# Layer 0's dense experts loaded as pairs of blocks of 1 MB, with the ring of gathered rows cut from 16 places to 14

## The chip, the cores and the metric

The kernel runs on one core of one Trainium2 chip. The metric is the device time of one execution in microseconds. A program on one core has that core as its slowest, so nothing is averaged over cores.

## What is computed

A diffusion backbone of two layers works on 256 latent tokens and 256 context tokens of 1024 features in float32. Each layer is a parallel mixer (two gated scans, two attentions) and then a feed-forward of 16384 small experts (PEER). Of the latter each token takes 8 x 16 = 128 experts:

```python
def peer_ffn(h, w_q, keys, u, v):
    ...
        best, sel = lax.top_k(cand, PEER_TOPK)
        eidx = jnp.take_along_axis(cidx, sel, axis=-1)
        g = jax.nn.softmax(best, axis=-1)
        act = jax.nn.gelu(jnp.einsum('td,thkd->thk', xb, u[eidx]).astype(jnp.float32))
        return jnp.einsum('thk,thkd->td', (g * act).astype(v.dtype), v[eidx]).astype(h.dtype)
```

In layer 0 this is done for the 256 context tokens and the 256 latent tokens, in layer 1 for the latent tokens alone.

## The kernel before

The change lies in `phase_mixed`, the feed-forward of layer 0, which runs two kinds of work beside each other.

**Dense, for the latent tokens.** All 16384 experts are gone through in 128 blocks of 128 experts. A block of `u` is 512 KB (`us`, 128 partitions x 1024 float32), and so is a block of `v` (`vs`). For block e: ScalarE copies the block to a rounded high part (`u_high`, L2328), VectorE subtracts to get the low part (`u_low`, L2363), TensorE makes 24 products (`hidden`), ScalarE applies gelu (L2337), VectorE multiplies by the gates (L2375) and makes another low part (L2382), the block of `v` is split in the same way (ScalarE L2346, VectorE L2384), and TensorE adds 24 products to the output (`outputs`). Each of `us` and `vs` has SW = 3 places of one block. The gates of four blocks come as one more transfer of 512 KB (L2235), in runs of 1 KB.

**Sparse, for the context tokens.** There are 512 gathers of 128 rows of 4 KB (512 KB each), listed in `order` and issued by GpSimd (L2251) into `ring`, which has R = 16 places. A row set of `u` is multiplied and summed by VectorE (a "dot", L2389). Four row sets of `v` together are used by TensorE in one "quad" (L2300). The list starts with the 128 `u` sets of token tile 0. Then come three `u` sets of tile 1 and one `v` set of tile 0 in turn, and then `v` sets alone. Slot s of the list may be gathered when slot s - R has been consumed.

All engines go through 132 steps. In step k TensorE does hidden(k), outputs(k - 2) and then, if one is due, a quad. VectorE does wt(k - 1), u_low(k + 1), wl and vl(k - 1), and then the dots of the four slots that belong to step k - 2 (PER = 4, LAG = 2). The first quad is due in step 37. In the part in which `u` and `v` sets alternate, one quad is due in every fourth step from there (37, 41, 45 and so on), and in the part with `v` sets alone one is due in each step.

SyncE's queue carries the dense loads in program order (L2229 u, L2235 gates, L2238 v), each behind a wait for the place it writes. It and GpSimd's queue share the core's 16 DMA engines.

The waits that matter for the order are these:

```python
if e >= SW:
    sp.wait_ge(vlo, e - SW + 1)
sp.dma_start(vs[:, e % SW], d["v_rows"][e * P:(e + 1) * P]).then_inc(v_in[e % SW], 16)
...
if s >= R:
    pool.wait_ge(*consumed(s - R))
```

Of the kernel before, what the change touches and what calls it, by code (L numbers as in the profile page):

```python
# [110 lines left out]
def f32(ap):  # L111

    return ap.bitcast(F32)
# [28 lines left out]
def build(nc, d, out):  # L142
# [14 lines left out]
    def sb(st, name, shape, dt=F32):  # L157
        return st.enter_context(nc.sbuf_tensor(name, shape, dt))

    with ctx:  # L160
# [1972 lines left out]
        def phase_mixed(l, hp, hT, eid, eidT, gate):  # L2133
# [6 lines left out]
            R = 16  # L2140
            PER = 4
            LAG = 2
            SW = 3
# [52 lines left out]
            with ExitStack() as st:  # L2196
                us = sb(st, f"peer_u{l}", [P, SW, DC, P])
                uh = sb(st, f"peer_uh{l}", [P, 2, DC, P], F32R)
                ul = sb(st, f"peer_ul{l}", [P, 2, DC, P], F32R)
                vs = sb(st, f"peer_v{l}", [P, SW, D_MODEL])  # L2200
# [22 lines left out]
                with nc.Block() as block:  # L2223
                    @block.sync
                    def _(sp):
                        for e in range(NKEY):
                            if e >= SW:
                                sp.wait_ge(ulo, e - SW + 1)
                            sp.dma_start(us[:, e % SW], d["uT"][e]).then_inc(u_in[e % SW], 16)  # L2229
                            if e % GROWS == 0:  # L2230
                                b = e // GROWS
                                if b >= 2:
                                    sp.wait_ge(w_done, GROWS * (b - 1))
                                src = gates_dram[0:ntb, :, e:e + GROWS, :].rearrange("b p i t -> p b (i t)")
                                sp.dma_start(gs[:, b % 2].rearrange("p b i t -> p b (i t)"), src).then_inc(g_in[b % 2], 16)  # L2235
                            if e >= SW:
                                sp.wait_ge(vlo, e - SW + 1)
                            sp.dma_start(vs[:, e % SW], d["v_rows"][e * P:(e + 1) * P]).then_inc(v_in[e % SW], 16)  # L2238
# [84 lines left out]
                    def _(act):  # L2323
                        def u_high(e):
                            act.wait_ge(u_in[e % SW], 16 * (e // SW + 1))
                            if e >= 2:
                                act.wait_ge(act_mm, e - 1)
                            nc.scalar.activation(uh[:, e % 2], us[:, e % SW], ACT.Copy).then_inc(uhi, 1)  # L2328

                        u_high(0)  # L2330
                        for step in range(steps + 1):
# [8 lines left out]
                            if 0 <= e < NKEY:  # L2340
                                act.wait_ge(w_done, e + 1)
                                if e >= 2:
                                    act.wait_ge(out_mm, e - 1)
                                nc.scalar.activation(wh[:, e % 2], wt[:, e % 2], ACT.Copy).then_inc(whi, 1)
                                act.wait_ge(v_in[e % SW], 16 * (e // SW + 1))
                                nc.scalar.activation(vh[:, e % 2], vs[:, e % SW], ACT.Copy).then_inc(vhi, 1)  # L2346
# [13 lines left out]
                    def _(dve):  # L2360
                        def u_low(e):
                            dve.wait_ge(uhi, e + 1)
                            nc.vector.tensor_tensor(ul[:, e % 2], us[:, e % SW], f32(uh[:, e % 2]), ALU.subtract).then_inc(ulo, 1)  # L2363

                        u_low(0)
                        for step in range(steps + 1):
# [13 lines left out]
                            if 0 <= e < NKEY:  # L2380
                                dve.wait_ge(whi, e + 1)
                                nc.vector.tensor_tensor(wl[:, e % 2], wt[:, e % 2], f32(wh[:, e % 2]), ALU.subtract).then_inc(wlo, 1)  # L2382
                                dve.wait_ge(vhi, e + 1)
                                nc.vector.tensor_tensor(vl[:, e % 2], vs[:, e % SW], f32(vh[:, e % 2]), ALU.subtract).then_inc(vlo, 1)  # L2384
# [127 lines left out]
def lay_out(x, c, ctx, c_ctx, ada_w, ada_b, norm_mix_g, norm_ffn_g, w_in, w_out,  # L2512
# [34 lines left out]
    a["uT"] = peer_u[0].reshape(NKEY, P, DC, P).transpose(0, 3, 2, 1)  # L2547
# [21 lines left out]
```

## Time and profile before

| | |
|---|---|
| median of 3 runs | 3184.79 us (3181.0 to 3188.43) |
| the profiled execution, its own time | 3183.49 us |
| its span | 3181.7 us |
| mean granted TensorE clock | 0.888 |
| TensorE matmul busy | 2546.1 us (80%) |
| VectorE busy | 2022.4 us (64%) |
| `phase_mixed` in the span | from about 980 to about 2045 us |

The page has a digit for each fortieth of the span (79.5 us): busy tenths of each engine, the granted clock and the busy share of the DMA engines. A share a little over 1 in the windows means that records of packets overlap.

### The profile page before, as it was taken

The page shows a single profiled execution, that of the slowest core. Times are in us where ns is not written, and L with a number is a line of the kernel's source. Part 1 is how long each engine was busy: PE and PEld are TensorE (multiplying, and loading weights), DVE is VectorE, ACT ScalarE, POOL GpSimd, SP SyncE. Part 2 cuts the span into 40 slices and gives each one's busy share as a digit, 9 for nine tenths or more (in the row PEclk, how much of TensorE's full clock was granted, in tenths as well). Part 3 has the DMA queues.
Part 4 walks back from the last instruction along what each step waited for, and adds up shares of the span by engine and source line. Part 5 has one row for each costly group of instructions (what it writes and reads, how often), then busy time and mean ns, then how long its engine had stood idle before and what let it go on. Part 6 is the DMA issues. An engine that isn't in the chain of part 4 may idle for free. (4 is left out here: it accounts for less than half of the span.)

```text
span 3181.7 us, 41584 instructions
## 1 busy us (share of the span) xinstructions
PE 2546.1 (80%) x15562; PEld 1903.4 (60%) x15562; DVE 2022.4 (64%) x4495; ACT 1084.4 (34%) x2179; POOL 1119.1 (35%) x1013
## 2 busy tenths in 40 slices
PE   5978699797376778878799999888877797777776
PEld 3778445595165777767777777577746553222222
DVE  3566435489995989887844333467543699845444
ACT  3422235321073333333333333342234443333332
POOL 1024100331005667556665555212302354433431
PEclk8985589897698989999999999988678899999999
DMA  5210141135238999999999999621002799999996
GB/s 208 74 30 1 62 159 42 53 113 180 106 152 325 405 407 404 363 401 385 402 406 406 405 406 406 263 87 43 9 1 85 303 391 422 421 421 422 421 422 258
DMA packets 211897, 816.93 MB, mean 257 GB/s; under 512 B 22681, under 2 KB 41689, under 8 KB 178033
## 3 DMA queue, kind: packets, MB, share of 16 engines
q0 software_dynamic: 110592, 536.92, 41.7%
q1 hardware_dynamic: 101104, 277.35, 23.4%
q8 instruction: 124, 2.03, 0.3%
q14 instruction: 77, 0.62, 0.1%
HBM read 796.37 MB, written 17.83 MB: 256 GB/s over the span
## 5 line engine op out<-in xcount | busy, mean ns | idle before, releaser
L1919 PE MATMUL ps<-pair_ring,pair_diag 128*128 128x512 f32 x1024 | 476.3, 610 | 144.8 <-ACT pair_diag L1993 142.2
L2103 DVE CUSTOM_DVE_ANT_0 pair_ring<-pair_ring,hT 128x1024 f32<-128x1024 f32 x256 | 312.9, 1222 | 206.7 <-DMA pair_ring<-in_uv_rows,eid 206.7
L1919 PEld LDWEIGHTS ps<-pair_ring,pair_diag 128*128 128x128 f32 x1024 | 187.1, 192 | 423.3 <-ACT pair_diag L1993 228.5
L1883 POOL DMA_INDIRECT pair_ring<-in_uv_rows,eid x256 | 268.2, 1048 | 391.9 <-PE ps L1919 364.0
L2251 POOL DMA_INDIRECT sparse_ring<-in_v_rows,eidT x256 | 279.5, 1092 | 298.4 <-PE ps L2300 226.9
L2251 POOL DMA_INDIRECT sparse_ring<-in_u_rows,eid x256 | 339.4, 1326 | 122.5 <-issue 68.1
L118 PE MATMUL ps<-h_hi,peer_uh 128*128 128x256 f32 x1024 | 310.1, 303 | 85.6 <-DVE peer_ul L2363 77.9
L2389 DVE CUSTOM_DVE_ANT_0 sparse_ring<-sparse_ring,hT 128x1024 f32<-128x1024 f32 x256 | 304.7, 1224 | 41.9 <-DMA sparse_ring<-in_u_rows,eid 35.7
L120 PE MATMUL ps<-h_hi,peer_ul 128*128 128x256 f32 x1024 | 299.2, 292 | 1.1 <-issue 0.9
L119 PE MATMUL ps<-h_lo,peer_uh 128*128 128x256 f32 x1024 | 299.4, 292 | 0.1
L118 PEld LDWEIGHTS ps<-h_hi,peer_uh 128*128 128x128 f32 x1024 | 206.0, 201 | 149.4 <-DVE peer_ul L2363 92.0
L118 PE MATMUL ps<-peer_wh,peer_vh 128*128 128x256 f32 x1024 | 291.3, 285 | 1.8 <-issue 1.7
L119 PE MATMUL ps<-peer_wl,peer_vh 128*128 128x256 f32 x1024 | 290.5, 284 | 0.4 <-issue 0.3
L120 PE MATMUL ps<-peer_wh,peer_vl 128*128 128x256 f32 x1024 | 290.1, 283 | 0.1
L2363 DVE TENSOR_TENSOR peer_ul<-peer_u,peer_uh 128x1024 fp32r<-128x1024 f32 x128 | 156.5, 1223 | 164.3 <-ACT peer_uh L2328 132.7
L2328 ACT ACTIVATE peer_uh<-peer_u 128x1024 fp32r<-128x1024 f32 x128 | 135.2, 1057 | 292.2 <-DMA peer_u<-in_uT 273.7
L120 PEld LDWEIGHTS ps<-h_hi,peer_ul 128*128 128x128 f32 x1024 | 206.2, 201 | 1.3 <-issue 1.3
L119 PEld LDWEIGHTS ps<-h_lo,peer_uh 128*128 128x128 f32 x1024 | 206.6, 202 | 0.2 <-issue 0.2
L118 PEld LDWEIGHTS ps<-peer_wh,peer_vh 128*128 128x128 f32 x1024 | 197.8, 193 | 2.6 <-issue 2.4
L119 PEld LDWEIGHTS ps<-peer_wl,peer_vh 128*128 128x128 f32 x1024 | 197.5, 193 | 2.1 <-issue 2.1
L120 PEld LDWEIGHTS ps<-peer_wh,peer_vl 128*128 128x128 f32 x1024 | 197.2, 193 | 0.8 <-issue 0.8
L2300 PE MATMUL ps<-sparse_ring,sparse_wdiag 128*32 128x512 f32 x1024 | 137.2, 653 | 67.2 <-DMA sparse_ring<-in_v_rows,eidT 66.2
(397 smaller groups left out, 5411.5 us busy)
## 6 DMA issues: line engine op xcount, KB each, us to landing
peer_u<-in_uT SPq DMA_DIRECT2D x128, 512.0 KB
peer_v<-in_v_rows SPq DMA_DIRECT2D x128, 512.0 KB
ada_slab<-in_ada_w SPq DMA_DIRECT2D x20, 2048.0 KB, 8.6
proj_slab<-in_w_fm SPq DMA_DIRECT2D x38, 512.0 KB
route_slab<-in_w_pq SPq DMA_DIRECT2D x32, 512.0 KB, 3.3
peer_gates<-dense_stage SPq DMA_DIRECT2D x4, 4096.0 KB, 13.1
peer_gates<-peer_gates SPq DMA_DIRECT2D x32, 512.0 KB
out_slab<-in_w_out SPq DMA_DIRECT2D x16, 512.0 KB, 3.7
```

The lines of the kernel that those rows point to most:

```text
L118: nc.tensor.matmul(out, w[0], x[0], start=start, stop=False)
L119: nc.tensor.matmul(out, w[0], x[1], start=False, stop=False)
L120: return nc.tensor.matmul(out, w[1], x[0], start=False, stop=stop)
L1883: nc.gpsimd.indirect_dma_start(out=ring[:, s % R], out_offset=None, in_=d["uv_rows"], in_offset=bass.IndirectOffsetOnAxis(ap=eid[:, s:s + ...
L1919: mm = nc.tensor.matmul(ps[:, 4 + 2 * t + half, :], diag[:, s % DG, :], ring[:, s % R, D_MODEL + half * BANK:D_MODEL + (half + 1) * BANK], ...
L2103: nc.vector.tensor_tensor_reduce(out=row, in0=row, in1=hT[:, s // NS], scale=1.0, scalar=0.0, op0=ALU.mult, op1=ALU.add, accum_out=dots[:, ...
L2251: nc.gpsimd.indirect_dma_start(out=ring[:, s % R], out_offset=None, in_=rows, in_offset=bass.IndirectOffsetOnAxis(ap=at, axis=0)).then_inc ...
L2300: mm = nc.tensor.matmul(ps[32 * q:32 * (q + 1), 6 + half, :], wdiag[:, q, j, :], ring[:, s % R, half * BANK:(half + 1) * BANK], start=(j = ...
L2328: nc.scalar.activation(uh[:, e % 2], us[:, e % SW], ACT.Copy).then_inc(uhi, 1)
L2363: nc.vector.tensor_tensor(ul[:, e % 2], us[:, e % SW], f32(uh[:, e % 2]), ALU.subtract).then_inc(ulo, 1)
L2389: nc.vector.tensor_tensor_reduce(out=ring[:, s % R], in0=ring[:, s % R], in1=hT[:, t], scale=1.0, scalar=0.0, op0=ALU.mult, op1=ALU.add, a ...
```

## The change

A block of `u` and the block after it become one transfer of 1 MB that writes 8 KB in each partition, and the same for `v`. For that the host lays `uT` out by pairs and adds an input `v_pairs` (the gathers go on reading `v_rows`). `us` and `vs` have two places of a pair each where they had three places of a block. So they take 8 KB more per partition in all, and the ring of gathered rows, 4 KB a place, gives these up: R is 14. SyncE waits until both blocks of the pair two before have been used. The arithmetic is the same.

```diff
-            R = 16
+            R = 14
...
-            SW = 3
+            SW = 2
...
-                us = sb(st, f"peer_u{l}", [P, SW, DC, P])
+                us = sb(st, f"peer_u{l}", [P, SW, 2, DC, P])
...
-                vs = sb(st, f"peer_v{l}", [P, SW, D_MODEL])
+                vs = sb(st, f"peer_v{l}", [P, SW, 2, D_MODEL])
...
-                        for e in range(NKEY):
-                            if e >= SW:
-                                sp.wait_ge(ulo, e - SW + 1)
-                            sp.dma_start(us[:, e % SW], d["uT"][e]).then_inc(u_in[e % SW], 16)
-                            if e % GROWS == 0:
-                                b = e // G**Rows 1.** The page, busy share in 40 slices of the span.

```profile
DMA  5210141135238999999999999621002799999996
GB/s 208 74 30 1 62 159 42 53 113 180 106 152 325 405 407 404 363 401 385 402 406 406 405 406 406 263 87 43 9 1 85 303 391 422 421 421 422 421 422 258
```

**Rows 2.** DMA of 980:2045, all of `phase_mixed`: queue, packets, MB, share of 16 engines.

```profile
DMA packets 127569, 420.62 MB, mean 395 GB/s; under 512 B 12800, under 2 KB 29184, under 8 KB 127488
...
q0 software_dynamic: 73728, 268.47, 63.6%
q1 hardware_dynamic: 53760, 151.01, 36.4%
```

**Rows 3.** Windows: us, busy (instructions) by engine, clock, DMA share, GB/s.

```profile
1064.00:1264.00 200.00, 156.50 (x1170) 152.24 (x1169) 183.90 (x292) 63.99 (x96) 135.50 (x97) 0.92 1.03 405
1300.00:1400.00 100.00, 81.02 (x621) 72.60 (x620) 83.33 (x125) 32.24 (x48) 60.11 (x49) 0.91 1.03 404
1400.00:1500.00 100.00, 80.67 (x624) 71.76 (x623) 79.48 (x120) 32.58 (x48) 59.74 (x48) 0.91 1.00 388
...
1800.00:1900.00 100.00, 95.53 (x778) 74.49 (x777) 38.12 (x48) 32.65 (x48) 51.56 (x51) 1.00 1.03 406
```

**Rows 4.** DMA of 2690:3100, layer 1, where gathered rows have 8 KB.

```profile
DMA packets 23716, 172.77 MB, mean 421 GB/s; under 512 B 2632, under 2 KB 2632, under 8 KB 2632
```

**Rows 5.** DMA of 1306:1322, between two transfers of gates, runs of 4 KB.

```profile
DMA packets 1798, 6.56 MB, mean 410 GB/s; under 512 B 199, under 2 KB 199, under 8 KB 1797
```

**Rows 6.** DMA of 616:640, with one transfer of 1024 KB over 128 partitions.

```profile
DMA packets 700, 3.06 MB, mean 128 GB/s; under 512 B 80, under 2 KB 80, under 8 KB 572
...
route_keys<-in_keysT SPq DMA_DIRECT2D x1, 1024.0 KB, 8.3
```

**Rows 7.** DMA of 1552:1554 and of 1556:1558, each queue's share.

```profile
q0 software_dynamic: 113, 0.41, 51.7%
q1 hardware_dynamic: 113, 0.40, 49.9%
...
q0 software_dynamic: 171, 0.61, 77.1%
q1 hardware_dynamic: 48, 0.20, 24.4%
```

**Rows 8.** Waits of 1060:1240: who waited for whom, us, times, longest.

```profile
ACT peer_uh L2328 <- DMA peer_u<-in_uT: 88.3, 22, 8.0
```

**Rows 9.** Window of 1284:1300, before the first quad, columns as in Rows 3.

```profile
1284.00:1300.00 16.00, 16.00 (x128) 14.43 (x128) 15.57 (x24) 7.40 (x12) 2.54 (x3) 0.95 0.56 193
```

**Rows 10.** Timelines of ACT, POOL, PE and SP, start us, us, [idle before <- releaser].

```profile
984.76 1.06 ACT L2328 ACTIVATE peer_uh<-peer_u 128x1024 fp32r<-128x1024 f32 x1 [17.52 <-DMA peer_u<-in_uT]
...
1296.85 0.95 POOL L2251 DMA_INDIRECT sparse_ring<-in_v_rows,eidT  x1 [20.53 <-PE ps L2300]
...
1315.94 1.93 POOL L2251 DMA_INDIRECT sparse_ring<-in_v_rows,eidT  x1 [0.30 <-issue]
...
1330.86 0.94 POOL L2251 DMA_INDIRECT sparse_ring<-in_v_rows,eidT  x1 [9.04 <-PE ps L2300]
...
1327.30 3.26 PE L2300 MATMUL ps<-sparse_ring,sparse_wdiag 128*32 128x512 f32 x16 [7.54 <-DMA sparse_ring<-in_v_rows,eidT]
...
1329.84 0.33 SPq L2238 DMA_DIRECT2D peer_v<-in_v_rows  x1
...
1595.39 0.94 POOL L2251 DMA_INDIRECT sparse_ring<-in_v_rows,eidT  x1 [8.61 <-PE ps L2300]
```

**Rows 11.** DMA of 1332:1334 and of 1334:1336, just after that quad.

```profile
q1 hardware_dynamic: 389, 0.75, 103.7%
q0 software_dynamic: 10, 0.03, 4.3%
...
q1 hardware_dynamic: 143, 0.49, 62.3%
q0 software_dynamic: 73, 0.29, 36.4%
```
-                                if b >= 2:
-                                    sp.wait_ge(w_done, GROWS * (b - 1))
-                                src = gates_dram[0:ntb, :, e:e + GROWS, :].rearrange("b p i t -> p b (i t)")
-                                sp.dma_start(gs[:, b % 2].rearrange("p b i t -> p b (i t)"), src).then_inc(g_in[b % 2], 16)
-                            if e >= SW:
-                                sp.wait_ge(vlo, e - SW + 1)
-                            sp.dma_start(vs[:, e % SW], d["v_rows"][e * P:(e + 1) * P]).then_inc(v_in[e % SW], 16)
+                        for b in range(NKEY // 2):
+                            if b >= SW:
+                                sp.wait_ge(ulo, 2 * (b - SW + 1))
+                            sp.dma_start(us[:, b % SW], d["uT"][b]).then_inc(u_in[b % SW], 16)
+                            if 2 * b % GROWS == 0:
+                                x = 2 * b // G**Rows 1.** The page, busy share in 40 slices of the span.

```profile
DMA  5210141135238999999999999621002799999996
GB/s 208 74 30 1 62 159 42 53 113 180 106 152 325 405 407 404 363 401 385 402 406 406 405 406 406 263 87 43 9 1 85 303 391 422 421 421 422 421 422 258
```

**Rows 2.** DMA of 980:2045, all of `phase_mixed`: queue, packets, MB, share of 16 engines.

```profile
DMA packets 127569, 420.62 MB, mean 395 GB/s; under 512 B 12800, under 2 KB 29184, under 8 KB 127488
...
q0 software_dynamic: 73728, 268.47, 63.6%
q1 hardware_dynamic: 53760, 151.01, 36.4%
```

**Rows 3.** Windows: us, busy (instructions) by engine, clock, DMA share, GB/s.

```profile
1064.00:1264.00 200.00, 156.50 (x1170) 152.24 (x1169) 183.90 (x292) 63.99 (x96) 135.50 (x97) 0.92 1.03 405
1300.00:1400.00 100.00, 81.02 (x621) 72.60 (x620) 83.33 (x125) 32.24 (x48) 60.11 (x49) 0.91 1.03 404
1400.00:1500.00 100.00, 80.67 (x624) 71.76 (x623) 79.48 (x120) 32.58 (x48) 59.74 (x48) 0.91 1.00 388
...
1800.00:1900.00 100.00, 95.53 (x778) 74.49 (x777) 38.12 (x48) 32.65 (x48) 51.56 (x51) 1.00 1.03 406
```

**Rows 4.** DMA of 2690:3100, layer 1, where gathered rows have 8 KB.

```profile
DMA packets 23716, 172.77 MB, mean 421 GB/s; under 512 B 2632, under 2 KB 2632, under 8 KB 2632
```

**Rows 5.** DMA of 1306:1322, between two transfers of gates, runs of 4 KB.

```profile
DMA packets 1798, 6.56 MB, mean 410 GB/s; under 512 B 199, under 2 KB 199, under 8 KB 1797
```

**Rows 6.** DMA of 616:640, with one transfer of 1024 KB over 128 partitions.

```profile
DMA packets 700, 3.06 MB, mean 128 GB/s; under 512 B 80, under 2 KB 80, under 8 KB 572
...
route_keys<-in_keysT SPq DMA_DIRECT2D x1, 1024.0 KB, 8.3
```

**Rows 7.** DMA of 1552:1554 and of 1556:1558, each queue's share.

```profile
q0 software_dynamic: 113, 0.41, 51.7%
q1 hardware_dynamic: 113, 0.40, 49.9%
...
q0 software_dynamic: 171, 0.61, 77.1%
q1 hardware_dynamic: 48, 0.20, 24.4%
```

**Rows 8.** Waits of 1060:1240: who waited for whom, us, times, longest.

```profile
ACT peer_uh L2328 <- DMA peer_u<-in_uT: 88.3, 22, 8.0
```

**Rows 9.** Window of 1284:1300, before the first quad, columns as in Rows 3.

```profile
1284.00:1300.00 16.00, 16.00 (x128) 14.43 (x128) 15.57 (x24) 7.40 (x12) 2.54 (x3) 0.95 0.56 193
```

**Rows 10.** Timelines of ACT, POOL, PE and SP, start us, us, [idle before <- releaser].

```profile
984.76 1.06 ACT L2328 ACTIVATE peer_uh<-peer_u 128x1024 fp32r<-128x1024 f32 x1 [17.52 <-DMA peer_u<-in_uT]
...
1296.85 0.95 POOL L2251 DMA_INDIRECT sparse_ring<-in_v_rows,eidT  x1 [20.53 <-PE ps L2300]
...
1315.94 1.93 POOL L2251 DMA_INDIRECT sparse_ring<-in_v_rows,eidT  x1 [0.30 <-issue]
...
1330.86 0.94 POOL L2251 DMA_INDIRECT sparse_ring<-in_v_rows,eidT  x1 [9.04 <-PE ps L2300]
...
1327.30 3.26 PE L2300 MATMUL ps<-sparse_ring,sparse_wdiag 128*32 128x512 f32 x16 [7.54 <-DMA sparse_ring<-in_v_rows,eidT]
...
1329.84 0.33 SPq L2238 DMA_DIRECT2D peer_v<-in_v_rows  x1
...
1595.39 0.94 POOL L2251 DMA_INDIRECT sparse_ring<-in_v_rows,eidT  x1 [8.61 <-PE ps L2300]
```

**Rows 11.** DMA of 1332:1334 and of 1334:1336, just after that quad.

```profile
q1 hardware_dynamic: 389, 0.75, 103.7%
q0 software_dynamic: 10, 0.03, 4.3%
...
q1 hardware_dynamic: 143, 0.49, 62.3%
q0 software_dynamic: 73, 0.29, 36.4%
```
+                                if x >= 2:
+                                    sp.wait_ge(w_done, GROWS * (x - 1))
+                                src = gates_dram[0:ntb, :, 2 * b:2 * b + GROWS, :].rearrange("b p i t -> p b (i t)")
+                                sp.dma_start(gs[:, x % 2].rearrange("p b i t -> p b (i t)"), src).then_inc(g_in[x % 2], 16)
+                            if b >= SW:
+                                sp.wait_ge(vlo, 2 * (b - SW + 1))
+                            sp.dma_start(vs[:, b % SW], d["v_pairs"][b]).then_inc(v_in[b % SW], 16)
...
-                            act.wait_ge(u_in[e % SW], 16 * (e // SW + 1))
+                            act.wait_ge(u_in[e // 2 % SW], 16 * (e // 2 // SW + 1))
...
-                            nc.scalar.activation(uh[:, e % 2], us[:, e % SW], ACT.Copy).then_inc(uhi, 1)
+                            nc.scalar.activation(uh[:, e % 2], us[:, e // 2 % SW, e % 2], ACT.Copy).then_inc(uhi, 1)
...
-    a["uT"] = peer_u[0].reshape(NKEY, P, DC, P).transpose(0, 3, 2, 1)
+    a["uT"] = peer_u[0].reshape(NKEY // 2, 2, P, DC, P).transpose(0, 4, 1, 3, 2)
+    a["v_pairs"] = peer_v[0].reshape(NKEY // 2, 2, P, D_MODEL).transpose(0, 2, 1, 3)
```

The other lines of the diff (L2346, L2363, L2384) only address the block inside its pair.

SyncE's program at the start of `phase_mixed` (`in_uT` is the input of `u`, `in_v_rows` that of `v`, `peer_gates` the gates), four blocks of it before:

```order
L2229 DMA peer_u<-in_uT 128x1024
L2235 DMA peer_gates<-peer_gates 128x4x256
L2238 DMA peer_v<-in_v_rows 128x1024
L2229 DMA peer_u<-in_uT 128x1024
L2238 DMA peer_v<-in_v_rows 128x1024
L2229 DMA peer_u<-in_uT 128x1024
L2238 DMA peer_v<-in_v_rows 128x1024
L2229 DMA peer_u<-in_uT 128x1024
L2238 DMA peer_v<-in_v_rows 128x1024
```

The same queue at the same place after the change:

```order
L2229 DMA peer_u<-in_uT 128x2048
L2235 DMA peer_gates<-peer_gates 128x4x256
L2238 DMA peer_v<-in_v_pairs 128x2048
L2229 DMA peer_u<-in_uT 128x2048
L2238 DMA peer_v<-in_v_pairs 128x2048
```

Four blocks take five transfers where they took nine, and the gates stand behind a pair of `u` and ahead of a pair of `v`. The programs of TensorE, VectorE and ScalarE have the same instructions in the same order, and so has GpSimd's; its waits look 14 slots back instead of 16.

## Rows read from the trace of the kernel before

**Rows 1.** The page, busy share in 40 slices of the span.

```profile
DMA  5210141135238999999999999621002799999996
GB/s 208 74 30 1 62 159 42 53 113 180 106 152 325 405 407 404 363 401 385 402 406 406 405 406 406 263 87 43 9 1 85 303 391 422 421 421 422 421 422 258
```

**Rows 2.** DMA of 980:2045, all of `phase_mixed`: queue, packets, MB, share of 16 engines.

```profile
DMA packets 127569, 420.62 MB, mean 395 GB/s; under 512 B 12800, under 2 KB 29184, under 8 KB 127488
...
q0 software_dynamic: 73728, 268.47, 63.6%
q1 hardware_dynamic: 53760, 151.01, 36.4%
```

**Rows 3.** Windows: us, busy (instructions) by engine, clock, DMA share, GB/s.

```profile
1064.00:1264.00 200.00, 156.50 (x1170) 152.24 (x1169) 183.90 (x292) 63.99 (x96) 135.50 (x97) 0.92 1.03 405
1300.00:1400.00 100.00, 81.02 (x621) 72.60 (x620) 83.33 (x125) 32.24 (x48) 60.11 (x49) 0.91 1.03 404
1400.00:1500.00 100.00, 80.67 (x624) 71.76 (x623) 79.48 (x120) 32.58 (x48) 59.74 (x48) 0.91 1.00 388
...
1800.00:1900.00 100.00, 95.53 (x778) 74.49 (x777) 38.12 (x48) 32.65 (x48) 51.56 (x51) 1.00 1.03 406
```

**Rows 4.** DMA of 2690:3100, layer 1, where gathered rows have 8 KB.

```profile
DMA packets 23716, 172.77 MB, mean 421 GB/s; under 512 B 2632, under 2 KB 2632, under 8 KB 2632
```

**Rows 5.** DMA of 1306:1322, between two transfers of gates, runs of 4 KB.

```profile
DMA packets 1798, 6.56 MB, mean 410 GB/s; under 512 B 199, under 2 KB 199, under 8 KB 1797
```

**Rows 6.** DMA of 616:640, with one transfer of 1024 KB over 128 partitions.

```profile
DMA packets 700, 3.06 MB, mean 128 GB/s; under 512 B 80, under 2 KB 80, under 8 KB 572
...
route_keys<-in_keysT SPq DMA_DIRECT2D x1, 1024.0 KB, 8.3
```

**Rows 7.** DMA of 1552:1554 and of 1556:1558, each queue's share.

```profile
q0 software_dynamic: 113, 0.41, 51.7%
q1 hardware_dynamic: 113, 0.40, 49.9%
...
q0 software_dynamic: 171, 0.61, 77.1%
q1 hardware_dynamic: 48, 0.20, 24.4%
```

**Rows 8.** Waits of 1060:1240: who waited for whom, us, times, longest.

```profile
ACT peer_uh L2328 <- DMA peer_u<-in_uT: 88.3, 22, 8.0
```

**Rows 9.** Window of 1284:1300, before the first quad, columns as in Rows 3.

```profile
1284.00:1300.00 16.00, 16.00 (x128) 14.43 (x128) 15.57 (x24) 7.40 (x12) 2.54 (x3) 0.95 0.56 193
```

**Rows 10.** Timelines of ACT, POOL, PE and SP, start us, us, [idle before <- releaser].

```profile
984.76 1.06 ACT L2328 ACTIVATE peer_uh<-peer_u 128x1024 fp32r<-128x1024 f32 x1 [17.52 <-DMA peer_u<-in_uT]
...
1296.85 0.95 POOL L2251 DMA_INDIRECT sparse_ring<-in_v_rows,eidT  x1 [20.53 <-PE ps L2300]
...
1315.94 1.93 POOL L2251 DMA_INDIRECT sparse_ring<-in_v_rows,eidT  x1 [0.30 <-issue]
...
1330.86 0.94 POOL L2251 DMA_INDIRECT sparse_ring<-in_v_rows,eidT  x1 [9.04 <-PE ps L2300]
...
1327.30 3.26 PE L2300 MATMUL ps<-sparse_ring,sparse_wdiag 128*32 128x512 f32 x16 [7.54 <-DMA sparse_ring<-in_v_rows,eidT]
...
1329.84 0.33 SPq L2238 DMA_DIRECT2D peer_v<-in_v_rows  x1
...
1595.39 0.94 POOL L2251 DMA_INDIRECT sparse_ring<-in_v_rows,eidT  x1 [8.61 <-PE ps L2300]
```

**Rows 11.** DMA of 1332:1334 and of 1334:1336, just after that quad.

```profile
q1 hardware_dynamic: 389, 0.75, 103.7%
q0 software_dynamic: 10, 0.03, 4.3%
...
q1 hardware_dynamic: 143, 0.49, 62.3%
q0 software_dynamic: 73, 0.29, 36.4%
```

More of the change, by code:

```diff
@@ L2225, in _ @@
                     def _(sp):
-                        for e in range(NKEY):
-                            if e >= SW:
-                                sp.wait_ge(ulo, e - SW + 1)
-                            sp.dma_start(us[:, e % SW], d["uT"][e]).then_inc(u_in[e % SW], 16)
-                            if e % GROWS == 0:
[L2231 to L2238, printed above, removed]
+                        for b in range(NKEY // 2):
+                            if b >= SW:
+                                sp.wait_ge(ulo, 2 * (b - SW + 1))
+                            sp.dma_start(us[:, b % SW], d["uT"][b]).then_inc(u_in[b % SW], 16)
+                            if 2 * b % GROWS == 0:
+                                x = 2 * b // GROWS
+                                if x >= 2:
+                                    sp.wait_ge(w_done, GROWS * (x - 1))
+                                src = gates_dram[0:ntb, :, 2 * b:2 * b + GROWS, :].rearrange("b p i t -> p b (i t)")
+                                sp.dma_start(gs[:, x % 2].rearrange("p b i t -> p b (i t)"), src).then_inc(g_in[x % 2], 16)
+                            if b >= SW:
+                                sp.wait_ge(vlo, 2 * (b - SW + 1))
+                            sp.dma_start(vs[:, b % SW], d["v_pairs"][b]).then_inc(v_in[b % SW], 16)
                     @block.gpsimd
@@ L2324, in u_high @@
                         def u_high(e):
-                            act.wait_ge(u_in[e % SW], 16 * (e // SW + 1))
+                            act.wait_ge(u_in[e // 2 % SW], 16 * (e // 2 // SW + 1))
                             if e >= 2:
                                 act.wait_ge(act_mm, e - 1)
-                            nc.scalar.activation(uh[:, e % 2], us[:, e % SW], ACT.Copy).then_inc(uhi, 1)
+                            nc.scalar.activation(uh[:, e % 2], us[:, e // 2 % SW, e % 2], ACT.Copy).then_inc(uhi, 1)
                         u_high(0)
@@ L2344, in _ @@
                                 nc.scalar.activation(wh[:, e % 2], wt[:, e % 2], ACT.Copy).then_inc(whi, 1)
-                                act.wait_ge(v_in[e % SW], 16 * (e // SW + 1))
-                                nc.scalar.activation(vh[:, e % 2], vs[:, e % SW], ACT.Copy).then_inc(vhi, 1)
+                                act.wait_ge(v_in[e // 2 % SW], 16 * (e // 2 // SW + 1))
+                                nc.scalar.activation(vh[:, e % 2], vs[:, e // 2 % SW, e % 2], ACT.Copy).then_inc(vhi, 1)
                             for t in range(nt):
@@ L2546, in lay_out @@
     a["keysT"] = peer_keys.reshape(DEPTH, 2 * PH, NKEY, P).transpose(0, 3, 1, 2)
-    a["uT"] = peer_u[0].reshape(NKEY, P, DC, P).transpose(0, 3, 2, 1)
+    a["uT"] = peer_u[0].reshape(NKEY // 2, 2, P, DC, P).transpose(0, 4, 1, 3, 2)
+    a["v_pairs"] = peer_v[0].reshape(NKEY // 2, 2, P, D_MODEL).transpose(0, 2, 1, 3)
     a["u_rows"] = peer_u[0]
```

4 lines of the change are left out of this document (2 added, 2 removed).

## The prediction

> **What bounds the kernel now.** I read the page first for the slices of `phase_mixed`, then the DMA queues of that stretch, then windows by stage, and last the waits and the timeline around the places where the DMA is not full. Between 980 and 2045 us the busy digit of the DMA engines is 9 in nearly every slice, at 401 to 407 GB/s where nothing dips [rows 1]. In that stretch they move 420.62 MB at a mean of 395 GB/s, 63.6% of their time for the gathers (q0) and 36.4% for SyncE's loads (q1) [rows 2]. VectorE is busy 184 of 200 us early and 38 of 100 us late, while the DMA share stays at 1.03 and the rate at 405 or 406 GB/s [rows 3]. So neither VectorE nor TensorE sets the pace of the whole phase. The bytes do: 420.62 MB at 406 GB/s are 1036 us of about 1065. A change pays here if it makes the bytes move faster or shortens the 29 us in which they don't move. It costs if it opens new gaps. I look for nothing outside this phase, since nothing else is edited.
>
> **The runs of 8 KB: -8.6 us.** In layer 1, where a gathered row has 8 KB, 421 GB/s are moved [rows 4]. Here, with runs of 4 KB in both queues and no gates in flight, it is 410 GB/s [rows 5]. SyncE's queue can make such runs too: with one transfer of 1024 KB over 128 partitions, 700 - 572 = 128 packets had 8 KB or more [rows 6]. The blocks of `u` and `v` are 256 x 0.524 = 134.2 MB. At 410 GB/s they take 327.4 us, at 421 GB/s 318.8 us, so 8.6 us are saved. The bounds are 0 (the packets stay at 4 KB, or the gathers' rate holds the pair back) and about 2 x 8.6 (the other queue gains as well). I take 8.6, since both rows are long and full. The Trainium skill ("DMA: Bandwidth & Descriptors", section "Why small descriptors are slow") charges some 3 cycles per packet beside one cycle per 32 bytes, which makes 259 cycles for 8 KB against 262 for two of 4 KB: by that 1.1%, an estimate of 3.7 us where the rows give 8.6. The rows differ by 2.7%, so I stay with them.
>
> **Fewer waits for u: nothing by itself.** ScalarE waits 88.3 us of 180 for a block of `u` [rows 8]. The reason is in how the queues share. With runs of 4 KB in both they have half each, and while gates in runs of 1 KB are on their way q0 has 77.1% and q1 24.4% [rows 7]. Those gates stand ahead of the next blocks in q1. With runs of 8 KB q1 should have two thirds while its blocks move, and the gates now come at the end of a burst, with nothing behind them for two steps. So u will be early and these waits should nearly go. But the DMA is full during them [rows 3], so what `u` gains the gathered rows lose: VectorE will wait for them instead. I cost this at 0, covered by the full DMA, with one exception, which is next. By the Trainium skill (same page, "Queues, rings and completion order") an engine goes round its queues packet by packet; the halves and the 77 to 24 above agree with that.
>
> **The gap before the first quad: -6 us.** From 1284 to 1300 only 193 GB/s are moved, that is (1 - 193/408) x 16 = 8.4 us of DMA time unused [rows 9]. All that the rings allow had landed: GpSimd stood 20.53 us until 1296.85 for the quad of step 37 [rows 10], and the engines were late because of the waits for `u` before. Now VectorE follows the gathers. The last slot of that quad (143) should land at about 1283 as before, since the DMA was always full up to 1284; with 3.3 us of quad [rows 10] GpSimd can go on at about 1288 instead of 1297. Some 8.5 us are won, of which two sets fewer in the ring take back 2 x 0.524 MB / 410 GB/s = 2.6 us. I take -6. The bounds are -8.4 (the gap gone) and +2.6 (engines as late as now, and two sets fewer landed).
>
> **The ring of 14 while u and v alternate: +18 us.** A quad takes slots that lie four apart, so its first place is held long: slot 147 cannot be gathered before the quad of step 37 is done, and with 14 places it is slot 145. Each such round of four steps runs as follows now. GpSimd resumes at T = 1330.86 after 9.04 us idle [rows 10]. The gathers move again only at about T + 3.7: they have 4.3% of 1332 to 1334 and 36.4% of the next 2 us, at half rate the last 1.4 us of these [rows 11]. In between q1 fills the engines (103.7%) with the load issued at 1329.84 and the gates before it [rows 10, 11]. The next quad needs the 13th set issued after the resumption before (issued at 1315.94, awaited until 1327.30). Nine rounds, from 1296.85 to 1595.39, are 33.2 us each [rows 10]; the bytes of a round, 25 x 0.524 = 13.1 MB, need 32.3 us at 406 GB/s. So the gap of q0 is nearly covered today, because the two sets issued before the stop are still on their way at T. With 14 places they are not issued. The gap begins 2.6 us sooner, and the quad needs 15 sets after T. What covers it is worse placed, too: the gates come with the burst two steps before (15 us), not one, and the pair's burst starts to move only some 3 us after its issue, at about T + 2. A round is then 3.7 us to the restart, 15 sets and 3.5 to 4.0 MB of dense loads at 412 GB/s (27.6 to 28.8 us), and 3.5 us for landing and quad: 34.8 to 36.0 us, or 1.6 to 2.8 more than 33.2. The bounds are 0 (pairs, whose two places hold a block more each, cover the gap wholly) and 2.8. I take 2.0, nearer the lower end of the working, since part of a burst may still be behind the quad's last set; nine rounds make +18 us. This already has the faster runs of the rounds, so of the 8.6 us above only what lies outside them is counted: 720 of 1065 us, -5.8.
>
> **The late part and the ends.** With `v` sets alone a quad frees four places in each step, and ten sets are still issued when TensorE waits for one; the DMA has always work: 0. ScalarE starts at 984.76 once the first 512 KB of `u` are there [rows 10]; 1 MB needs 0.524 / 0.41 = 1.3 us more. GpSimd fills the ring meanwhile, so I take +1, between 0 and +2.6. SyncE issues 128 loads fewer; its queue stands waiting most of the time: 0.
>
> **Sum.** -5.8 - 6 + 18 + 1 = +7.2 us. The profiled execution took 3183.5 us, 1.3 less than the median of the runs, 3184.8. So 3190.7 there, and 3192.0 for a median. A measurement of this kernel can tell about 0.2% (6.4 us) from no change, and 7.2 us is 0.23%: just outside.
>
> **Rivals.**
> - *The dense bursts cover the gap (faster).* Two places of a pair hold one block more than three places of a block, for `u` and for `v`, exactly what the ring lost. A burst is due in every second step and a quad in every fourth, and VectorE's burst of step k + 1 falls just at T, so 2 MB wait there where 1 MB did. The dips of today (388 GB/s in 1400 to 1500 [rows 3]) could then even shrink. For it: q1 covers the gap today [rows 11]. Against it: q1 will be done sooner after each burst. The third term is then 0 and the first whole: -8.6 - 6 + 1 = -13.6, about 3171; with the first gap unchanged, -7.6, about 3177.
> - *Rows starved by the bursts (slower, more than forecast).* At T the two sets that VectorE needs next meet a burst of 2 MB that takes two thirds. Each set then takes 0.524 / 0.137 = 3.8 us, and VectorE stands some 7 us per round. It has about 28 us of work in a round of 33 (83% [rows 3]), so with 7 us of standing it needs 35 us and from there on it decides itself. If that adds 1 us to the 2.8 in nine rounds, the sum is -5.8 - 3 + 34 + 1 = +26, 3211.
> - *No runs of 8 KB.* If the loads are cut to 4 KB, the rate stays and the queues go on sharing by halves: the first terms go, and the ring's remains, about +12 to +18, 3200. Rows 6 speak against it.
> - *The terms cancel.* With 1 us more per round in place of 2 (+9) the sum is -2, 3183.
>
> **How the numbers follow.** The forecast case, +3 to +20 us, has 0.35; starved rows 0.08; no long runs 0.03; terms that cancel 0.26; covered gaps 0.28. The part of the first under 6.4 us (0.06) counts as the same, as does 0.01 of the covered case. So faster 0.27, same 0.33, slower 0.40. The range reaches from the covered case to past the forecast: 3171 to 3207, with one tenth left out on each side. The forecast case's own range is 3188 to 3205.
>
> **What would show it.** Right steps: 512 packets of 8 KB per four blocks in q1 (two pairs of u, two of v) and a rate of 412 to 416 GB/s where the DMA is full; ScalarE's wait for `u` nearly gone and VectorE's wait for gathered rows in its place; GpSimd released for the first time near 1288 to 1290; then rounds of about 35 us with a hole of some 3 us in the DMA just before and after each release. Wrong: rounds of 33 us or less without a hole (the bursts cover it, and the kernel is faster), the rate at 406, or VectorE full between 1300 and 1600 us.

## The result and the profile after

In the diff of SyncE's program the two lines that break off at `G` divide by the number of blocks whose gates come in one transfer, four: `e // 4` before and `2 * b // 4` after.

The median of 7 runs is 3198.18 us (3190.47 to 3219.98), where 7 runs of before gave 3184.79 us (3181.0 to 3188.43). The ratio of after to before is 1.0057, with a 95% interval of 1.003 to 1.0084. The span of the profiled execution is 3194.8 us, before 3181.7.

The change makes the kernel slower: by 13.4 us between the medians, by 0.57% (18 us) in the ratio, which the slowest of its runs pull up, and by 13.1 us between the two profiled executions. The runs of after spread over 30 us, those of before over 7.

Put on the time axis, the 13.1 us split at three marks. GpSimd's first release by a quad comes at 1289.26 us (before 1296.85 [rows 10]): -7.6. Its release nine rounds later comes at 1614.31 (before 1595.39 [rows 10]), so a round takes (1614.31 - 1289.26) / 9 = 36.1 us in place of 33.2: +26.5 over nine. From there to the first addition of the outputs (L1349, at 2041.58 before and at 2058.44 now) -2.1 us are won, and in the rest of the kernel, where nothing was edited, -3.8. That rest took from 1134.8 to 1142.7 us in the thirteen profiled executions of this case, whatever the kernel, so -3.8 says nothing of the change. The marks in the timelines after the change:

| mark | engine | start, us | idle before, us | ended by |
|---|---|---|---|---|
| first release by a quad | GpSimd (L2251) | 1289.26 | 24.43 | TensorE's quad (L2300) |
| release nine rounds later | GpSimd (L2251) | 1614.31 | 10.81 | TensorE's quad (L2300) |
| first addition of the outputs | VectorE (L1349) | 2058.44 | 7.15 | TensorE's products (L120) |

The windows by stage after the change, from the same view as [rows 3]:

| window, us | TensorE busy, us | VectorE busy, us | clock | DMA share | GB/s |
|---|---|---|---|---|---|
| 1064 to 1264 | 160.06 | 190.54 | 0.94 | 1.03 | 410 |
| 1284 to 1300 | 13.29 | 7.46 | 1.00 | 0.81 | 313 |
| 1300 to 1400 | 74.80 | 76.30 | 0.90 | 0.94 | 365 |
| 1400 to 1500 | 80.44 | 73.31 | 0.90 | 0.95 | 371 |
| 1800 to 1900 | 97.91 | 41.64 | 1.00 | 1.03 | 410 |

Where the DMA is full, it is faster: 410 in place of 405 and 406 GB/s early and late. The hole before the first quad has shrunk, 313 in place of 193 GB/s [rows 9]. But in the part where `u` and `v` sets alternate the rate has fallen from 404 and 388 to 365 and 371, and VectorE is less busy there, not more (76 of 100 us where it was 83). So VectorE's work is not the new bound; the time goes where few or no bytes move. The page counts 193463 packets where there were 211897, 18434 fewer. The pairs should take away 16384 runs and 2048 completions (128 transfers by 16), 18432 in all.

One such hole, the window of 4 us just before GpSimd's release at 1397.98, columns as in [rows 3]:

```profile
1394.00:1398.00 4.00, 3.96 (x18) 1.07 (x19) 3.60 (x5) 1.20 (x2) 0.02 (x1) 0.53 0.27 76
```

The 4 us before it move 399 GB/s and the 4 us behind it 395.

From 1394 to 1398 only 76 GB/s are moved, so some 3.3 of the 4 us are lost. Up to 1394 TensorE has nothing to do; it waits for the fourth set of its quad. Then the quad runs, SyncE issues its burst (a pair of `v` and a pair of `u`) at 1396.48 and GpSimd its next gather at 1397.98, and VectorE stands for the row that this gather brings: 7.62 us, until 1405.22.

Over 1300 to 1600 us VectorE waits 54.9 us for gathered rows of `u`, where it waited 34.8 before.

How the queues share now shows in the DMA view of 1424 to 1426, a pair against gathers: SyncE's queue (q1) has 74 packets, 0.58 MB and 69.2%, the gathers' (q0) 69 packets, 0.26 MB and 32.9%. A pair of 8 KB runs gets two thirds where blocks had half [rows 7]. The gates are treated as before (27.8% to 76.7% from 1392 to 1394). The waits of 1060 to 1240 have lost ScalarE's 88.3 us for `u` [rows 8] altogether. ScalarE now waits 114.3 us for VectorE's L2375 (21 times, the longest 7.5 us; 34.9 us before), and VectorE, which waited for no row there, waits a little: 9.4 us in 13 waits of at most 1.9 us.

### The profile page after: what moved, and what is told of

It is laid out like the page before. It is cut to its first block and busy times, and to the rows that moved or that the text cites. A ratio compares the mean times of both kernels' runs of the same rounds, so it can differ in the third digit from the quotient of the medians.

```text
span 3194.8 us, 41456 instructions
## 1 busy us (share of the span) xinstructions
PE 2557.8 (80%) x15562; PEld 1906.6 (60%) x15562; DVE 2021.5 (63%) x4495; ACT 1077.3 (34%) x2179; POOL 1130.0 (35%) x1013
## 2 busy tenths in 40 slices
DMA packets 193463, 816.91 MB, mean 256 GB/s; under 512 B 20632, under 2 KB 39640, under 8 KB 143216
## 5 line engine op out<-in xcount | busy, mean ns | idle before, releaser
L2251 POOL DMA_INDIRECT sparse_ring<-in_u_rows,eid x256 | 325.9, 1273 | 245.7 <-PE ps L2300 136.2
L1883 POOL DMA_INDIRECT pair_ring<-in_uv_rows,eid x256 | 271.4, 1060 | 385.5 <-PE ps L1919 357.4
L2251 POOL DMA_INDIRECT sparse_ring<-in_v_rows,eidT x256 | 301.7, 1178 | 188.9 <-PE ps L2300 123.8
L120 PE MATMUL ps<-h_hi,peer_ul 128*128 128x256 f32 x1024 | 300.3, 293 | 0.3 <-issue 0.2
L120 PE MATMUL ps<-peer_wh,peer_vl 128*128 128x256 f32 x1024 | 290.3, 284 | 4.7 <-issue 4.5
L120 PEld LDWEIGHTS ps<-h_hi,peer_ul 128*128 128x128 f32 x1024 | 206.9, 202 | 1.8 <-issue 1.7
L2344 ACT ACTIVATE peer_wh<-peer_wt 128x256 fp32r<-128x256 f32 x128 | 53.4, 417 | 443.4 <-DVE peer_wt L2375 296.7
L120 PEld LDWEIGHTS ps<-peer_wh,peer_vl 128*128 128x128 f32 x1024 | 197.1, 193 | 5.1 <-issue 5.1
L2363 DVE TENSOR_TENSOR peer_ul<-peer_u,peer_uh 128x1024 fp32r<-128x1024 f32 x128 | 156.4, 1223 | 51.1 <-ACT peer_uh L2328 34.8
L2300 PE MATMUL ps<-sparse_ring,sparse_wdiag 128*32 128x512 f32 x1024 | 135.5, 650 | 65.2 <-DMA sparse_ring<-in_v_rows,eidT 64.7
## 6 DMA issues: line engine op xcount, KB each, us to landing
peer_u<-in_uT SPq DMA_DIRECT2D x64, 1024.0 KB
peer_v<-in_v_pairs SPq DMA_DIRECT2D x64, 1024.0 KB
peer_gates<-dense_stage SPq DMA_DIRECT2D x4, 4096.0 KB, 13.1
```

What stands on the lines that cost most here:

```text
L120: return nc.tensor.matmul(out, w[1], x[0], start=False, stop=stop)
L1883: nc.gpsimd.indirect_dma_start(out=ring[:, s % R], out_offset=None, in_=d["uv_rows"], in_offset=bass.IndirectOffsetOnAxis(ap=eid[:, s:s + ...
L2251: nc.gpsimd.indirect_dma_start(out=ring[:, s % R], out_offset=None, in_=rows, in_offset=bass.IndirectOffsetOnAxis(ap=at, axis=0)).then_inc ...
L2300: mm = nc.tensor.matmul(ps[32 * q:32 * (q + 1), 6 + half, :], wdiag[:, q, j, :], ring[:, s % R, half * BANK:(half + 1) * BANK], start=(j = ...
L2363: nc.vector.tensor_tensor(ul[:, e % 2], us[:, e // 2 % SW, e % 2], f32(uh[:, e % 2]), ALU.subtract).then_inc(ulo, 1)
```

## The experiments

The theory: with 14 places the gathers' queue runs dry some 2.6 us earlier in each round, and what is left of the dense loads doesn't fill the hole. The pairs themselves bring a little. Rivals: the pairs' bursts do the harm and the ring is innocent; or VectorE has become the bound.

| kernel | order of gathers | loads | ring | median, us | ratio to before (95%) | round, us | GB/s, 1325 to 1575 |
|---|---|---|---|---|---|---|---|
| before | alternate | blocks | 16 | 3184 to 3187 | | 33.2 | 396 |
| ring15_blocks | alternate | blocks | 15 | 3191.78 | 1.0032 (1.0019 to 1.0044) | 34.6 | 382 |
| ring14_blocks | alternate | blocks | 14 | 3203.68 | 1.0046 (1.0029 to 1.0064) | 35.6 | 374 |
| ring14_blocks_again | alternate | blocks | 14 | 3205.65 | 1.0063 (1.005 to 1.0076) | 35.9 | 366 |
| the change | alternate | pairs | 14 | 3198.18 | 1.0057 (1.003 to 1.0084) | 36.1 | 366 |
| pairs14_again | alternate | pairs | 14 | 3201.19 | 1.0058 (1.0044 to 1.0073) | 35.3 | 368 |
| pairs13 | alternate | pairs | 13 | 3202.42 | 1.0069 (1.0054 to 1.0083) | 36.3 | 367 |
| pairs14_shift1 | alternate, one step later | pairs | 14 | 3207.24 | 1.0064 (1.0051 to 1.0076) | 36.9 | 352 |
| upairs_vblocks16 | alternate | u pairs, v blocks | 16 | 3178.55 | 0.9982 (0.9973 to 0.9991) | 33.7 | 391 |
| blocks16_grouped | 12 u, 4 v | blocks | 16 | 3168.80 | 0.9943 (0.9931 to 0.9956) | | 405 |
| pairs14_grouped_4k | 12 u, 4 v | pairs, 4 KB runs | 14 | 3168.79 | 0.9956 (0.9943 to 0.9968) | 32.8 | 406 |
| pairs14_grouped | 12 u, 4 v | pairs | 14 | 3164.57 | 0.9932 (0.9919 to 0.9945) | 32.2 | 410 |
| pairs12_grouped | 12 u, 4 v | pairs | 12 | 3161.68 | 0.9929 (0.9916 to 0.9942) | 32.2 | 410 |

A round is the mean of nine in one profiled execution, between GpSimd's releases by a quad, read as in [rows 10]. In blocks16_grouped most of GpSimd's stops end with VectorE's dots, so it has no such round. The same kernel read twice gives 35.6 and 35.9 (ring14_blocks) and 36.1 and 35.3 (the change): differences under a microsecond tell little.

**The ring alone.**

```diff
-            R = 16
+            R = 14
```

> Only the ring of the kernel before is cut to 14 places; u and v stay in blocks of 512 KB with three places. Theory (the ring opens the gap, and the burst's timing decides how much of it is covered): the first release of GpSimd stays near 1297 us, since the waits for u are as before, and the rounds of four steps after it grow from 33.2 to 34.2 to 34.7 us, because gates and a block pair of loads still fall just before the release and cover part of the 2.6 us; with 2.6 us for two sets fewer at the first release, +12 to +16 us, about 3199. Rival 1 (the pairs' bursts are at fault, the ring is harmless): rounds of 33.2 us and the time within 3 us of before. Rival 2 (the ring alone explains all): rounds of 36 us as in the changed kernel and, without the faster runs of 8 KB and with the old first release, +35 us, 3220.

Rounds of 35.6 us, 3203.7 us. Rival 1 falls: the ring alone makes the kernel slower by about as much as the whole change. The total of +16.6 us between the medians is the theory's, but by another way: it expected rounds of 34.2 to 34.7 us. Blocks and gates cover no more of the hole than pairs do, so the rounds are nearly those of rival 2, without its +35 us. The first release came at 1292.40, 4.5 us earlier than before and not near 1297; in ring14_blocks_again it came at 1296.39, so it varies by 4 us in one kernel.

**One place less.**

```diff
-            R = 16
+            R = 15
```

> The kernel before with a ring of 15 places, blocks of 512 KB as before. With 16 places a round of four steps took 33.2 us, with 14 (ring14_blocks) 35.6. Theory (each place missing starts the gap of the gathers' queue one set, 1.28 us, earlier, and nothing else covers it): 34.3 to 34.5 us per round, and about half of what 14 places cost, +6 to +9 us. Rival (a threshold between 14 and 16: either the first set missing costs nothing or it costs all): rounds of 33.2 or of 35.6 us.

34.6 us per round and 7.3 us more than before by the medians, as expected. No threshold: 33.2, 34.6, 35.6 for 16, 15 and 14 places, 1.2 us per place on average, where a set of 0.524 MB at 410 GB/s is 1.28 us.

**The order of the gathers, with pairs.** `order` is the list in which GpSimd gathers and the others consume:

```diff
-                order += u1[:PER - 1] + v0[:1]
-                u1, v0 = u1[PER - 1:], v0[1:]
+                order += u1[:12] + v0[:4]
+                u1, v0 = u1[12:], v0[4:]
```

> The changed kernel with another order of the same gathers: where three u sets and one v set took turns, twelve u sets and then four v sets do. A quad's four places then lie together and no place is held over four steps. Theory (held places make the gap): GpSimd's stops of 10 to 15 us vanish, rounds of four steps take 31.8 to 32.5 us instead of 36.1, the DMA is full at about 410 GB/s from 1300 to 1600 us, and the kernel takes 34 to 39 us less than the changed one, about 3161, some 24 less than before. Rival (bursts of 8 KB runs starve the rows, or VectorE with four dots in each of three steps is the bound): rounds stay at 34 us or more, 3180 or more.

The theory holds: rounds of (1577.04 - 1286.86) / 9 = 32.2 us, stops of GpSimd of 3.6 to 7.2 us, and 33.6 us less than the changed kernel by the medians, just under the 34 to 39 expected. In this kernel the DMA is full through the part that had the holes:

```profile
1325.00:1575.00 250.00, 208.99 (x1616) 187.81 (x1618) 206.47 (x312) 83.23 (x126) 159.10 (x125) 0.93 1.02 410
```

VectorE does 206 of 250 us there, more than the 180 of the changed kernel, so it was not the bound. With the same ring, the same bursts and the same two thirds for them (67.3% to 33.8% from 1342 to 1344), the holes are gone. What made them is that a quad's four places lay four slots apart, so that its first place was held over four steps.

**The same order without pairs.** The same four lines in the kernel before.

> The kernel before with the order of twelve u sets and four v sets; ring 16, blocks of 512 KB. It tells what the order is worth without pairs. Theory: the gap of today is nearly covered, so the rounds go from 33.2 only to 32.3 to 32.6 us: -5 to -8 us, about 3178. What then lies between this and the same order with pairs is what the pairs are worth: 8.6 us of faster runs and about 8 us at the first release, 12 to 18 us in all. Rival (the order frees much more, since even 16 places were short): 3165 or less, and the pairs worth under 5 us.

3168.8 us, 0.57% (18 us) less than before, where I had expected 5 to 8 us. I had counted the rounds alone. The order also closes the hole before the first quad, which in the kernel before is 310 GB/s from 1264 to 1300 us, here 406: 36 x (1 - 310/406) = 8.5 us. So 16 places were short there too, as the rival says, though its 3165 wasn't reached. And since the order takes that hole, the pairs no longer can: they are worth some 4 us in this order, not 12 to 18.

**The length of the runs.** The kernel pairs14_grouped with inputs laid out by blocks: the transfers and places are the same, and a transfer reads runs of 4 KB. The lines of the host's part (in the kernel only the access patterns of the two loads change with them):

```diff
+    a["uT"] = peer_u[0].reshape(NKEY // 2, 2, P, DC, P).transpose(0, 1, 4, 3, 2)
+    a["v_pairs"] = peer_v[0].reshape(NKEY // 2, 2, P, D_MODEL)
```

> The kernel pairs14_grouped (twelve u sets, then four v sets) with the same transfers of 1 MB into the same places, but the inputs laid out by blocks, so that a transfer reads runs of 4 KB. It tells apart what the length of the runs gives from what larger transfers with two places give. Theory (the runs make the rate): the DMA moves 406 GB/s where it moved 410, packets of 8 KB vanish from SyncE's queue, both queues share by halves again, and the time is 7 to 10 us more than pairs14_grouped, 3172 to 3175. Rival (the runs give nothing; fewer and larger transfers or the order do): within 2 us of pairs14_grouped at 410 GB/s.

The DMA view of 1300 to 1600 us:

| kernel | packets | of these under 8 KB | MB | GB/s |
|---|---|---|---|---|
| pairs14_grouped_4k | 36278 | 36255 | 121.85 | 406 |
| pairs14_grouped | 31898 | 27218 | 122.89 | 410 |

So packets of 8 KB and more go from 4680 (31898 - 27218) to 23. With 4 KB runs the queues share by halves again: from 1332 to 1334 SyncE's has 54.3% and the gathers' 47.7%.

The long runs make 406 into 410 GB/s; the larger transfers don't. The first addition of the outputs comes at 2028.23 with 4 KB runs and at 2018.87 with 8 KB runs, 9.4 us earlier, close to the 8.6 us of the prediction. In the medians it is 4.2 us, below the 7 to 10 expected, and the intervals of the two ratios overlap slightly. The part behind that mark, which is the same in both, took 1137.6 and 1142.7 us in these two executions, which takes 5.1 us of it back. Fewer and larger transfers by themselves, at 3168.79 us, give what blocks gave.

**Pairs without the price.** u in pairs, v in blocks with two places, so that all 16 places stay. SyncE's program becomes (`load_u` loads a pair and, if due, its gates, with the waits of the changed kernel):

```diff
+                        load_u(0)
+                        for b in range(NKEY // 2):
+                            if b + 1 < NKEY // 2:
+                                load_u(b + 1)
+                            for e in (2 * b, 2 * b + 1):
+                                if e >= SW:
+                                    sp.wait_ge(vlo, e - SW + 1)
+                                sp.dma_start(vs[:, e % SW], d["v_rows"][e * P:(e + 1) * P]).then_inc(v_in[e % SW], 16)
```

> Pairs for u alone (two places of a pair, 16 KB per partition), v in blocks of 512 KB with two places (8 KB): 24 KB as in the kernel before, so the ring keeps its 16 places. The order of gathers is the old one; SyncE loads the next pair of u and its gates ahead of the two blocks of v. Theory (pairs are good, the ring was the price): rounds of 33 us or a little less, half of the gain in rate (4 us) and 3 to 6 us at the first release: -5 to -10 us, about 3177. Rival 1 (bursts themselves cost as much as they bring, ring apart): within 3 us of before. Rival 2 (two places are too few for v, and ScalarE stands for it): slower than before by 5 us or more, with waits of ScalarE on v in the list.

6 us less than before in the medians, interval 0.9973 to 0.9991, within the 5 to 10 expected, so both rivals fall. With all 16 places a kernel with pairs is faster and not slower: the ring was the price. The first release is at 1290.33. The four executions with pairs and the old list have it at 1286.80 to 1290.60, the four with blocks at 1292.40 to 1296.85 (the shifted list apart, whose first quad is due a step later), so an earlier first release belongs to the loads and not to the ring. Rounds took 33.7 us, half a microsecond more than before and not the 33 or less expected, which is within what one kernel varies.

**Where the burst falls.** One step of u sets is put ahead of the alternate part, so quads fall in even steps.

```diff
+            order, u1 = order + u1[:PER], u1[PER:]
             while u1:
```

> The changed kernel with one step of u sets alone added before the alternate part, so that the quads fall in steps 38, 42, 46 and so on, while the bursts of 2 MB stay in the even steps: a burst is issued some 8 us before each release instead of at the release. Ring, sizes and pairs are the same. Theory (the burst's place decides what of the gap is covered): rounds of 33.2 to 34.5 us, 14 to 26 us less than the changed kernel, 3172 to 3184. Rival (only the number of places counts): rounds of 36 us and the time of the changed kernel within 4 us.

The theory of the burst's place falls: rounds of 36.9 us, and 3207 us. That is 9 us more than the changed kernel, so the rival's "within 4 us" isn't met either. The burst does start earlier: it is issued at 1401.61, 6.6 us ahead of the release at 1408.22, and covers the time up to the release. The hole then opens behind it. Windows of this kernel around that release:

| window, us | TensorE busy, us | VectorE busy, us | GpSimd busy, us | DMA share | GB/s |
|---|---|---|---|---|---|
| 1404 to 1408 | 3.29 | 4.00 | 0.00 | 1.03 | 425 |
| 1408 to 1412 | 4.00 | 1.15 | 3.17 | 0.62 | 214 |
| 1412 to 1416 | 4.00 | 1.82 | 3.08 | 0.90 | 328 |

Bytes that are moved before the release are not there after it. And when nothing but fresh gathers is left, the rate is what GpSimd issues: from 1408.22 to 1420.76 it issues eight gathers, 8 x 0.524 MB / 12.54 us = 334 GB/s, and the last of these windows moves 328 GB/s.

**One place fewer with pairs.** R = 13 in the changed kernel.

> The changed kernel with 13 places instead of 14. Theory (one set more missing): rounds of 36.1 + 1.3 = 37.4 us and the first release 1 to 2 us later, together +12 to +15 us against the changed kernel, near 3212. Rival (with pairs the round is set by VectorE's work and its stops, not by the ring): rounds of 36 us, within 4 us of the changed kernel.

The theory missed: 36.3 us per round against 36.1 and 35.3 of the two kernels with 14, and 1.2 to 4.2 us more in the medians. The rival's number is right, its reason is not, since VectorE is busy only 181 of 250 us. In the round from 1433.30 to 1469.03 the second burst is issued at 1454.50, 21.2 us after the release, where the changed kernel has 19.4 (1417.33 after 1397.98). A later burst leaves more of itself for the hole, which may be what pays for the missing set. That is read from one round each and not tested, so it stays open why this place cost less than expected.

**The pairs alone.** The changed kernel and the ring of 14 with blocks, once more, this time side by side.

> The changed kernel once more, on the same chip and in the same rounds as a ring of 14 with blocks, to read what the pairs alone are worth under the old order of gathers. Theory (with the gap of the ring open, the rate of 410 in place of 406 GB/s saves bytes' time only outside the rounds, and the burst at the release covers no more than blocks and gates did): 3 to 8 us less than ring14_blocks_again, about 3198. Rival (at 14 places the bursts starve the next rows, and cost what the runs bring): within 2 us, or more than ring14_blocks_again.

> The kernel before with 14 places and blocks, as in ring14_blocks, for the comparison with pairs14_again. Expected where it was: about 15 us more than before, 3200 to 3204, with rounds of 35.6 us.

3201.2 against 3205.7 us: the pairs bring 4.5 us by the medians, within what I expected, though the two intervals overlap for the most part, so it isn't shown clear of noise. The first release is at 1290.60 against 1296.39. The ring with blocks took 21.4 us more than before, where about 15 was expected, with rounds of 35.9 us.

**Fewer places in the new order.** R = 12 in pairs14_grouped.

> The kernel pairs14_grouped (twelve u sets, then four v sets, pairs) with a ring of 12 places only. Theory (places count only while a place is held over four steps; without that 12 places are still 3 steps of rows, and the DMA has always something to do): within 4 us of pairs14_grouped, 3163 to 3169, with the DMA at 405 GB/s or more from 1300 to 1600 us. Rival (each place is worth 5 to 8 us, as from 16 to 14 in the old order): 3175 or more.

3161.7 us, 0.7% less than before and the fastest median of all (its interval overlaps that of pairs14_grouped), with two places fewer than the changed kernel. The rival's 3175 falls. In this order the places of the ring have no price down to 12. This version beats both kernels.

## Why the prediction was right, and where not

The median of 3198.18 us lies inside the range and 6 us above the forecast, and the direction was the likeliest of the three. The mechanism was the one forecast: a ring of 14 opens a hole around each release, and it costs more than the pairs bring. That the total came so near is in part luck: the rounds cost 8.5 us more than forecast, and 3.8 us of that were given back in a part that the change doesn't touch. By its steps:

- **The runs of 8 KB.** Right in size: 410 GB/s in place of 405 or 406. 286.4 MB at 406 and 134.2 MB at 421 GB/s make 410.7. By the 1.1% that the Trainium skill's charge per packet gives ("DMA: Bandwidth & Descriptors", "Why small descriptors are slow"), it would be 407.4, an estimate. The measured 410 decides for the rows. I had asked for 412 to 416 as a sign, which was more than my own term gives. Of the 5.8 us outside the rounds 2.1 are seen after the rounds; the rest can't be told from the gain at the first release.
- **Waits for u worth nothing by themselves.** Right: 88.3 us of them vanished, and the stretch was bound by bytes before (405 GB/s) and after (410).
- **The gap before the first quad.** -6 expected, with the release at 1288; it came at 1289.26, 7.6 us earlier. The first release also came earlier in upairs_vblocks16 with 16 places, so the loads cause it, as argued. Since it varies by 4 us in one kernel, the last microseconds of this are chance.
- **The ring of 14.** The step that failed in size: rounds of 34.8 to 36.0 us were worked out, and I took +2.0 a round from the lower half, "since part of a burst may still be behind the quad's last set". Measured are 36.1, +2.9 a round and +26.5 in place of +18: just past the upper end of the working, so the choice of 2.0 was wrong and not the sum behind it. The two kernels with blocks show that the ring does this alone. In the round from 1397.98 the gathers move again after 4.0 us (3.7 in the working), the quad starts 27.9 us after that (27.6 to 28.8), and its release comes 3.9 us later (3.5), 35.9 in all. The burst starts to move sooner than the 3 us after its issue that the working took, and just as the release comes: issued at 1396.48, it carries 0.08 MB up to 1398 and 0.76 MB from 1398 to 1400. It fills the time after the release and leaves that before it open. And the working took 412 GB/s for all bytes from the restart to the quad, where 396 GB/s were moved. The loss is in the middle of it: 412 GB/s from 1402 to 1414, 371 from 1414 to 1424 and 408 from 1424 to 1430. What the working left out fits the shifted kernel: GpSimd issues its sixteen gathers of this round from 1397.98 to 1421.94, one in 1.5 us on average or 350 GB/s, so once what had gathered before the restart is moved, the queue gives less than 410 until the next burst. No run with faster issue was made, so this part is read from the traces and not tested.
- **Late part and ends.** +1 was expected at the start. From the start to the first release there is no sign of a loss, and -3.8 us came in a part that the change doesn't touch. Its cause is open.
- **The rivals.** Covered gaps didn't happen; one burst at the release covers what blocks and gates did, no more. Starved rows did happen, as forecast in size (VectorE stands 7.62 us at 1405.22), but not in the way forecast: the gathers don't crawl at a third of the rate, they stand still until 1402, and from 1404 to 1418 they have the engines nearly to themselves. And it is no bound: TensorE then still waits 7.60 us for its own row, before the quad at 1429.90.

Why the runs of the changed kernel spread over 30 us stays open. Its rounds vary from 33.1 to 39.6 us within one execution, those before from 30.8 to 34.6.

## What to carry to other kernels

A ring's depth counts from the place that is held longest: while the oldest place waits, all behind it must wait too. So before places are traded for larger transfers, look at which consumer holds one longest. Here an order of the same work that lets four places go together was worth about 34 us against the changed kernel (3164.57 to 3198.18), while the larger transfers were worth about 4. When a resource is full on average, ask at each stop of the engine that feeds it what is left in the queues at that moment: a queue whose load is merely moved earlier covers nothing.

## What the runs showed of the hardware

- Two queues that are both busy share the DMA engines by packets, not by bytes: 4 KB against 4 KB gives halves [rows 7], 8 KB against 4 KB 69.2% to 32.9%, and 1 KB against 4 KB 27.8% to 76.7%. The counts of packets in these windows are close to equal: 113 and 113, 74 and 69, 190 and 166. So longer runs in one queue take rate from the other at once. That agrees with the turn by packets that the Trainium skill describes ("DMA: Bandwidth & Descriptors", "Queues, rings and completion order").
- One queue of gathers alone, just released, ran at 328 GB/s, though each gather moves 512 KB. GpSimd issued eight in 12.54 us (0.94 to 1.93 us each and 0.30 us between two), which is 334 GB/s. With gathers piled up behind a burst the same queue alone moved 0.85 MB in 2 us (1406 to 1408 in the changed kernel). A stop of this queue costs not only the stop.
